# The last stage of a two-block kernel: GpSimd adds a token's two expert rows, VectorE adds the sum to h

## The reference, cut to what matters

```
def hierarchical_moe(h, ...):
    ...
    y = lax.map(expert_block, (block_e, x_rows)).reshape(n_rows, D_)
    out = jnp.zeros((n_tok + 1, D_), h.dtype).at[row_tok].add(y * row_w[:, None])[:n_tok]
    return out.reshape(B_, L_, D_)

def second_block(...):
    ...
        h = h + hierarchical_moe(rmsnorm(h, ffn_norm[layer]), ...)
    ...
    return rmsnorm(h, final_norm)[:, N_META:]
```

## Time and profile before

| | us |
|---|---|
| median of 3 runs | 2124.89 |
| lowest and highest of them | 2114.44, 2128.37 |
| the profiled execution | 2122.15 |
| its span | 2120.4 |
| TensorE busy in it | 1957.2 (92%) |
| VectorE busy | 803.3 (38%) |
| ScalarE busy | 525.7 (25%) |
| GpSimd busy | 196.3 (9%) |
| first load of the last stage issued at | 2079.54 |

### The profile page before, as it was taken

How to read it: one execution, slowest core, us unless ns; L and a number is a source line. 1 busy time by engine, 2 the same in 40 slices (tenths; PEclk the granted TensorE clock), 3 DMA queues, 4 the chain that set the end, 5 groups by cost and what they waited for, 6 DMA issues and landing times. The chain is left out here.

```text
span 2120.4 us, 30533 instructions
## 1 busy us (share of the span) xinstructions
PE 1957.2 (92%) x12181; PEld 1110.7 (52%) x12181; DVE 803.3 (38%) x1885; ACT 525.7 (25%) x1270; POOL 196.3 (9%) x289
## 2 busy tenths in 40 slices
PE   8999999889998997999988999999999997999990
PEld 4545554478643883433335656677675564334330
DVE  1114565866443454211215533434343126111115
ACT  1003233433211320111133433333332110111112
POOL 0000002001153210111100000000000000111100
PEclk9999999989998988999998999999999997999995
DMA  3100100020021127999975000000010007799976
GB/s 139 62 24 20 40 21 4 1 82 4 2 81 50 45 95 327 379 424 424 414 294 204 23 0 1 1 1 1 1 80 14 40 40 312 305 423 425 416 327 261
DMA packets 45030, 307.82 MB, mean 145 GB/s; under 512 B 9120, under 2 KB 9440, under 8 KB 24768
## 3 DMA queue, kind: packets, MB, share of 16 engines
q1 hardware_dynamic: 31776, 267.48, 31.0%
q0 software_dynamic: 13104, 38.29, 4.6%
HBM read 282.34 MB, written 35.72 MB: 150 GB/s over the span
## 5 line engine op out<-in xcount | busy, mean ns | idle before, releaser
L243 PE MATMUL psum<-arena 64*64 64x64 f32 (+12 forms) x10850 | 1813.9, 411 | 95.7 <-issue 40.4
L243 PEld LDWEIGHTS psum<-arena 128*128 128x128 f32 (+4 forms) x10850 | 965.7, 158 | 893.4 <-issue 794.3
L2248 DVE TENSOR_TENSOR arena<-psum,arena 128x256 f32<-128x256 f32 x44 | 18.7, 425 | 393.1 <-ACT arena L2300 393.1
L1556 ACT ACTIVATE arena<-arena 128x1024 f32<-128x1024 f32 x43 | 45.4, 1056 | 244.2 <-DVE arena L2996 105.6
L2909 ACT ACTIVATE arena<-psum,arena 128x1024 f32<-128x1024 f32 (+8 forms) x72 | 50.2, 698 | 188.7 <-DVE arena L2945 188.7
L2300 ACT ACTIVATE arena<-psum 128x256 f32<-128x256 f32 x44 | 16.9, 383 | 302.4 <-PE psum L243 302.4
L2338 POOL DMA_INDIRECT arena<-xn_rows,arena x44 | 44.8, 1018 | 487.4 <-PE psum L2213 268.9
L1257 ACT ACTIVATE arena<-psum 128x256 f32<-128x256 f32 (+3 forms) x128 | 43.9, 355 | 103.5 <-PE psum L243 92.4
L2343 POOL DMA_INDIRECT expert_rows<-arena x44 | 44.1, 1003 | 214.7 <-ACT arena L2291 185.4
L2291 ACT ACTIVATE arena<-psum,arena 128x512 f32<-128x512 f32 x44 | 30.2, 687 | 134.0 <-PE psum L243 134.0
L2938 DVE TENSOR_TENSOR psum<-psum,arena 128x128 f32<-128x128 f32 (+2 forms) x72 | 20.4, 283 | 103.4 <-PE psum L243 103.0
(11 more groups left out here) (309 smaller groups left out, 1300.0 us busy)
## 6 DMA issues: line engine op xcount, KB each, us to landing
arena<-in_w_exp SPq DMA_DIRECT2D x64, 2048.0 KB, 23.0
arena<-in_w_exp SPq DMA_DIRECT2D x64, 1024.0 KB, 23.5
arena<-expert_rows SPq DMA_DIRECT2D x16, 1024.0 KB, 7.1
arena<-in_x SPq DMA_DIRECT2D x16, 512.0 KB, 4.1
xn_rows<-arena SPq DMA_DIRECT2D x16, 512.0 KB, 2.6
arena<-in_w_out SPq DMA_DIRECT2D x8, 512.0 KB, 7.9
arena<-in_w_o SPq DMA_DIRECT2D x1, 4096.0 KB, 12.4
out<-arena SPq DMA_DIRECT2D x8, 512.0 KB, 4.0
```

Of the source, the lines that this page charges most:

```text
L243: return e.matmul(out, lhsT, rhs, start=start, stop=stop, skip_group_check=True)
L1556: return e.activation(junk, h[:, s, :], ACT.Square, accum_out=sq_sum[:, s:s + 1])
```

## The change

For tiles 1 to 7, GpSimd adds row 1 to row 0 in the buffer `c_fin` and signals `fin_pair`; VectorE waits for that and adds the sum to h with one instruction. Tile 0 stays with VectorE, two adds, with row 1 first. The signal that h of a tile is complete (`fin_h`) now goes up once a tile and not twice; ScalarE and SP wait for the corresponding count. The loads and stores, their order and all buffers are as before.

```
+        fin_pair, fin_h = signal("final_pair"), layers[1].h_out
+
+        def pool_final(e):
+            for s in range(1, NT):
+                c = c_fin[s % 4]
+                e.wait_ge(*m_cf[s])
+                e.tensor_tensor(c[:, 0, :], c[:, 0, :], c[:, 1, :], ALU.add).then_inc(*fin_pair.up())
+
         def dve_final(e):
             for d, s in turns(NT, 3):
                 if d == 0:
-                    dve_combine(e, layers[1], s, c_fin[s % 4], m_cf[s])
+                    c = c_fin[s % 4]
+                    if s:
+                        e.wait_ge(*fin_pair.at(s))
+                    else:
+                        e.wait_ge(*m_cf[s])
+                        e.tensor_tensor(h[:, s, :], h[:, s, :], c[:, 1, :], ALU.add).then_inc(*V.up())
+                        e.wait_ge(*V.last())
+                    e.tensor_tensor(h[:, s, :], h[:, s, :], c[:, 0, :], ALU.add).then_inc(*fin_h.up())
...
         def act_final(e):
...
-                    e.wait_ge(*layers[1].h_out.at(2 * s + 2))
+                    e.wait_ge(*fin_h.at(s + 1))
...
         def sp_final(e):
...
-                    e.wait_ge(*layers[1].h_out.at(2 * s + 2))
+                    e.wait_ge(*fin_h.at(s + 1))
...
             pool_moe(e, layers[1])
+            pool_final(e)
```

## The result

The changed kernel takes 2127.43 us (median of 20 runs, 2119.07 to 2135.23), the kernel before 2120.57 us (median of 20, 2113.45 to 2128.37). The ratio is 1.0032, with a 95% interval of 1.0021 to 1.0043: slower by 6.8 us, between 4.5 and 9.1, and inside the 1% that was called no change.

A forecast was written before the change was run, and what follows sets the result against it. VectorE was taken to bound the last stage, transfers close behind. Removed -8.7, added +16.5, overlaps -1.9 and -1.0 gave +4.9 us, taken as +5: 2127.2 on the profiled run, 2129.9 on the median, so 2128, range 2117 to 2137.

The forecast's parts named there:

- What bounds the kernel: Last stage: VectorE leads at 3.79 us a tile, with transfers close behind at 3.76 us.
- Exclusion of GpSimd's adds and VectorE's two-input instructions: Last stage: a GpSimd add and a VectorE instruction with two on-chip inputs block each other; chance 0.80 with slipping in.
- the three held GpSimd instructions of the earlier trace: Evidence for blocking: GpSimd instructions started inside VectorE's add or scan ended only 0.04 to 0.11 us after it.
- The predicted marks: Expected profile: VectorE's add or normalization at 2 us and more beside GpSimd's adds, those partly longer than 2.36 us.
- The sum: Last stage: removed adds -8.7 us, added adds +16.5, overlaps -1.9 and -1.0, together +4.9 us.
- the overlap, -1.9 and -1.0: Part of a blocked instruction already passed: 0.27 us for each of seven on VectorE, about 0.17 for six on GpSimd.
- Who waits: Last stage: delayed normalizations delay stores and the loads behind them, load 5 by about 3 us, but add no term.
- the even 4.5 us a tile: Expected pace in the middle of the last stage, in place of 3.79 us.
- the 350 GB/s expected: Expected bandwidth in the middle of the last stage, down from 418 GB/s.
- Rival 1: Last stage: no blocking, transfers become the bound, -2.9 us, 2119.3 or on the median 2122.0; chance 0.10.
- Rival 2: Last stage: GpSimd gets the port only when VectorE runs dry, +9.2 us, 2131.4 or on the median 2134.1; chance 0.10.
- Against which time: Whole kernel: the sum gives 2127.2 on the profiled 2122.15 us and 2129.9 on the median; 2128 was chosen between.

The follow-up runs named there:

- e11: e10 with GpSimd's adds given back to VectorE, so both adds of every tile there; first landing of the last stage to end 33.8 us.
- e12: e10 with the load of tile s + 4 issued ahead of the store of tile s - 1; first landing to end 31.4 us, ratio 0.9995.
- e2: Kernel before plus seven GpSimd adds that read the norm's weights and that nobody waits for; first landing to end 45.1 us, ratio 1.005.
- e1: Kernel before plus fourteen GpSimd memsets into an unused buffer; first landing of the last stage to end 34.1 us, as before.
- e9: e7 plus seven GpSimd adds that read the norm's weights and write an unused buffer; first landing of the last stage to end 50.2 us.
- e10: Changed kernel with h copied to psum by ScalarE ahead of time; first landing of the last stage to end 35.1 us, ratio 0.9993.
- e5: Changed kernel with loads issued ahead of stores in SP's queue; first landing of the last stage to end 39.8 us, ratio 1.0033.
- e7: Kernel before with TensorE summing h and both rows in psum instead of VectorE; first landing to end 49.1 us, ratio 1.0075.
- e3: Changed kernel with each GpSimd add split into two of 128x512; first landing of the last stage to end 39.6 us.

## Why the prediction was right, point by point

**What bounds the kernel.** Right: VectorE, with the transfers close behind. e11 keeps VectorE's 3.79 us a tile and, but for 0.2 us, W; e12 takes seven of VectorE's adds away and ends 2.7 us earlier, not 8.7.

**Exclusion of GpSimd's adds and VectorE's two-input instructions.** Right, and now shown from three sides: e2 (+11.0 us with no wait added), e1 (0 with memsets), e9, e10 and e12 (none with an input in psum). One reading behind it was looser than it was put: of the three held GpSimd instructions of the earlier trace rows two waited behind VectorE's add and one behind its scan, so only two show "this very VectorE form". The predicted marks, records of 2 us and more on VectorE and a GpSimd add over 2.36 us, are all there.

**The sum.** +4.9 us forecast, +6.3 in the trace, 6.8 (4.5 to 9.1) in the runs. The removed and the added work were sized rightly (1.24 and 2.35). What was mis-sized is the overlap, -1.9 and -1.0. VectorE hides 0.15 to 0.20 us behind GpSimd and not 0.27, which had been read from another form of instruction; and behind the first and the last GpSimd add no VectorE instruction was waiting, of which a part could have passed meanwhile: VectorE stood 2.43 and 2.23 us for them, 4.66 where the sum had 4.0. The five others cost 10.2 us where it had 9.6. Together they are the missing 1.3 us.

**Who waits.** The load of tile 7 was called no added term. It was late (issued at 2108.01, landed 8.6 us later) and left GpSimd idle for 4.39 us and VectorE for 2.23. e5 takes that wait away and gains 0.6 us, since a held normalization (1.9 us) comes in its place; so the term was small but not nothing. The pace was not the even 4.5 us a tile that I had drawn. It is 6.6 us while both have data (2093.17 to 2099.74 to 2106.31), then 2.5 us while GpSimd waits for a load; over the eight normalizations it is 4.19 us against 3.48 before, the 0.7 us a tile of the forecast. The bandwidth in the middle fell below the 350 GB/s expected: 236, 229, 272 and 317 GB/s in the four stretches of 4 us from 2095 to 2111.

**Rival 1** (no blocking) doesn't happen here, but e10 and e12 made it happen. Under SP's old order, which the rival had, W is 1.0 us longer than before (e10) where it said -2.9: its assumption of three stores ahead of the last load and 418 GB/s throughout failed. e12's -2.7 comes near the figure with another order of the loads, which is in part luck.

**Rival 2** (GpSimd gets its turn only when VectorE is dry) is refuted: the third GpSimd add gets in between a normalization and an add that follow without a gap. It said 9.2 us.

**Against which time.** The kernel before has a median of 2120.57 us over 20 runs, below both bases that I used (2122.15 and 2124.89). The forecast of 2128 comes so near the measured 2127.43 by luck: its basis (2128 less the 4.9 us of the sum) was 2.5 us too high, and the sum 1.9 us too low against the runs (1.4 against the trace).

## What to carry to other kernels

Before moving a VectorE instruction to GpSimd, look at the inputs on both sides: when GpSimd reads on-chip memory and VectorE's instructions beside it have both inputs there, the two took turns in this kernel, and what moves is replaced by something almost twice as long (2.36 for 1.24 us). Putting one of VectorE's inputs in psum removed the exclusion (e10, e12). When the stage's next bound, here the transfers, lies 3 us behind, even a perfect offload is worth only that, so work that bound out first.

## What the runs showed of the hardware that was not expected

- A GpSimd add of 128 x 1024 that reads one tensor as both inputs and writes another buffer took 1.89 us (e9); one that reads two tensors and writes into one of them took 2.35 (e10, e12). Which of the two differences counts was not separated.
- Transfers ran at 311 to 346 GB/s for 8 us with their engines busy (e10), at 432 before and at 414 after. The cause is open.
- A float32 product of 128 x 512 is two recorded matmuls, 0.43 us each at the high clock and about 0.8 at a granted clock of 0.57.
- TensorE's granted clock rose from 0.50 after 3.0 us of matmuls in e7 and after 5.1 in e9, with 13.3 and 13.5 us without work ahead of them. The cause is open.
- Taking turns is by instruction: with halves of 1.27 us, VectorE's records fall from 3.36 and 3.18 us to 2.29 and 2.10 (e3).
